# Neighbourhood attention of a two-block model: score and value matmuls of two heads issued in turn on the two halves of the array

## What is computed

```python
s_loc = jnp.einsum('bcqhd,brcmhd->bhcqrm', q_r, kb)          # 256 band keys
s_loc = jnp.where(col_valid, s_loc + bias, NEG_INF)
s_ctx = jnp.einsum('bcqhd,blhd->bhcql', q_r, kc)             # 256 context keys
p = jax.nn.softmax(jnp.concatenate([s_loc, s_ctx], -1), -1)
out = einsum(p_loc, vb) + einsum(p_ctx, vc)
```

## Time and profile before

| | us |
|---|---|
| median of 3 runs | 1833.73 |
| lowest, highest | 1828.89, 1835.4 |
| the profiled execution, whole | 1830.14 |
| its span, first to last instruction | 1828.5 |

### The profile page before, as it was taken

The page is one execution under the profiler, slowest core; times in us unless marked ns, Lnnn a source line. Parts: engine busy times, 40 slices in busy tenths (PEclk is TensorE's granted clock), DMA queues, the critical chain, the costliest instruction groups (busy, mean ns, idle before and its releaser), DMA issues.

```text
span 1828.5 us, 22256 instructions
## 1 busy us (share of the span) xinstructions
PE 1789.1 (98%) x8184; PEld 1441.1 (79%) x8184; DVE 973.3 (53%) x1237; ACT 676.2 (37%) x945; POOL 187.5 (10%) x170
## 2 busy tenths in 40 slices
PE   8999999999999999999999999989999999999999
PEld 6888888877887777876888888866787777788887
DVE  4333358866764664556433333346867768654442
ACT  4232222244344355534323222135444445632221
POOL 0000001122204602012000000003010020000000
PEclk9999999988999999999999999999999999999999
DMA  5232346613112334222322233221222222133331
GB/s 201 92 103 92 102 161 206 200 36 119 56 58 70 116 115 153 77 69 71 114 93 102 93 102 100 100 76 64 90 92 67 92 77 81 46 127 106 103 105 67
DMA packets 50315, 182.68 MB, mean 100 GB/s; under 512 B 5648, under 2 KB 5904, under 8 KB 50000
## 3 DMA queue, kind: packets, MB, share of 16 engines
q1 hardware_dynamic: 44352, 161.50, 26.5%
q10 hardware_dynamic: 4896, 14.96, 2.4%
q0 software_dynamic: 1008, 5.41, 0.9%
HBM read 179.75 MB, written 2.10 MB: 99 GB/s over the span
## 4 chain that ended last, share of the span: by engine, by line
PE 90%; DVE 5%; ACT 2%; issue 2%; DMA 0%; DVEq 0%; ACTq 0%
PE proj L364 79%; PE aux L467 2%; PE aux L1334 1%; DVE w_lo L356 1%; PE aux L1316 1%; PE aux L1324 1%; PE aux L1133 1%; ACT w_hi L349 1%; DVE y L1490 1%; PE aux L690 1%; PE proj L1154 1%; PE aux L1317 1%; DVE h L502 1%; DVE a_lo L506 0%; ACT md L812 0%
## 5 line engine op out<-in xcount | busy, mean ns | idle before, releaser
L356 DVE TENSOR_TENSOR w_lo<-raw,w_hi 128x1024 fp32r<-128x1024 f32 x304 | 405.4, 1335 | 457.4 <-ACT w_hi L349 450.4
L364 PE MATMUL proj<-a_hi,w_hi 128*128 128x512 f32 x1504 | 597.1, 397 | 16.3 <-DVE a_lo L1839 8.9
L364 PE MATMUL proj<-a_hi,w_lo 128*128 128x512 f32 x1504 | 588.4, 391 | 0.0
L364 PE MATMUL proj<-a_lo,w_hi 128*128 128x512 f32 x1504 | 588.2, 391 | 0.0
L349 ACT ACTIVATE w_hi<-raw 128x1024 fp32r<-128x1024 f32 x304 | 319.8, 1053 | 283.4 <-PE proj L364 245.4
L364 PEld LDWEIGHTS proj<-a_hi,w_hi 128*128 128x128 f32 x1504 | 284.1, 189 | 86.2 <-issue 25.9
L364 PEld LDWEIGHTS proj<-a_lo,w_hi 128*128 128x128 f32 x1504 | 284.2, 189 | 60.5 <-issue 2.6
L364 PEld LDWEIGHTS proj<-a_hi,w_lo 128*128 128x128 f32 x1504 | 283.9, 189 | 59.8
L364 PE MATMUL proj<-hid_hi,w_lo 128*128 128x512 f32 x352 | 139.0, 395 | 0.0
L364 PE MATMUL proj<-hid_hi,w_hi 128*128 128x512 f32 x352 | 139.0, 395 | 0.0
L364 PE MATMUL proj<-hid_lo,w_hi 128*128 128x512 f32 x352 | 139.0, 395 | 0.0
(11 more groups left out here) (295 smaller groups left out, 2067.6 us busy)
## 6 DMA issues: line engine op xcount, KB each, us to landing
raw<-stream SPq DMA_DIRECT2D x304, 512.0 KB, 3.4
ctxk<-ada_in ACTq DMA_DIRECT2D x12, 512.0 KB, 3.5
ctxv<-ada_in ACTq DMA_DIRECT2D x12, 512.0 KB, 3.4
h<-x_in SPq DMA_DIRECT2D x4, 512.0 KB, 7.1
out<-h ACTq DMA_DIRECT2D x8, 256.0 KB, 2.0
btab<-rpb_in POOLq DMA_DIRECT2D x4, 384.0 KB, 3.5
side<-mem_in POOLq DMA_DIRECT2D x1, 1024.0 KB, 5.0
side<-ctx_in POOLq DMA_DIRECT2D x1, 1024.0 KB, 6.2
```

Of the source, the lines that this page charges most:

```text
L356: nc.vector.tensor_tensor(w_lo[:, st.slot], raw[:, st.slot], w_hi[:, st.slot].bitcast(F32), ALU.subtract).then_inc(lo_ready, 1)
L364: mm = nc.tensor.matmul(dst, a, b, start=start and n == 0, stop=stop and n == 2)
```

## The change

`scores(u)` becomes `scores_of_pair(u)`, which issues the band matmuls of head 0 and head 1 and then their context matmuls. It stands where scores(a+2) stood; scores(a+3), which stood behind turn(a+1), is gone from there. The pair waits for the exps of both earlier units instead of one at each. `values(u)` becomes `values_of_pair(u)`, which goes over the four blocks and issues head 0 and head 1 for each. Its wait is for the later of the two units' turned. No matmul is added or taken away, and the lists of DVE, ACT, POOL and SP are the same.

```diff
-            def scores(u):
-                cb, lo = u // 2, HD * (u % 2)
-                part = slice(lo, lo + HD)
+            def scores_of_pair(u):
+                cb = u // 2
+                heads = [slice(0, HD), slice(HD, 2 * HD)]
                 if u == 0:
...
-                if u >= 2:
-                    pe.wait_ge(u_exp, u - 1 + UN * i)
-                q = nq[part, cb * P:(cb + 1) * P]
-                nc.tensor.matmul(aux[:, u % 2, :M], q, grid(nk[part], ROWS, BAND_AT[cb], BAND), start=True, stop=True)
-                nc.tensor.matmul(aux[:, u % 2, M:], q, ck_c[part], start=True, stop=True).then_inc(u_sc, 1)
+                else:
+                    pe.wait_ge(u_exp, u + UN * i)
+                at = slice(cb * P, (cb + 1) * P)
+                for n, part in enumerate(heads):
+                    nc.tensor.matmul(aux[:, n, :M], nq[part, at], grid(nk[part], ROWS, BAND_AT[cb], BAND), start=True,
+                                     stop=True)
+                for n, part in enumerate(heads):
+                    nc.tensor.matmul(aux[:, n, M:], nq[part, at], ck_c[part], start=True, stop=True).then_inc(u_sc, 1)
...
-            def values(u):
-                cb, lo = u // 2, HD * (u % 2)
-                pe.wait_ge(u_pt, u + 1 + UN * i)
+            def values_of_pair(u):
+                cb = u // 2
+                pe.wait_ge(u_pt, u + 2 + UN * i)
...
                 for b in range(4):
-                    v = vband[:, 2 * cb + b, lo:lo + HD] if b < 2 else cv_c[:, b - 2, lo:lo + HD]
-                    mm = nc.tensor.matmul(aux[lo:lo + HD, 3, cb * P:(cb + 1) * P], v, npt[:, u % 2, b * P:(b + 1) * P],
-                                          start=(b == 0), stop=(b == 3))
-                mm.then_inc(u_pv, 1)
+                    for n in range(2):
+                        lo = HD * n
+                        v = vband[:, 2 * cb + b, lo:lo + HD] if b < 2 else cv_c[:, b - 2, lo:lo + HD]
+                        mm = nc.tensor.matmul(aux[lo:lo + HD, 3, cb * P:(cb + 1) * P], v,
+                                              npt[:, n, b * P:(b + 1) * P], start=(b == 0), stop=(b == 3))
+                        if b == 3:
+                            mm.then_inc(u_pv, 1)
...
                 if 8 <= j <= 11:
-                    values(a - 2)
-                    values(a - 1)
+                    values_of_pair(a - 2)
                 if 6 <= j <= 9:
-                    scores(a + 2)
+                    scores_of_pair(a + 2)
                 if 7 <= j <= 10:
                     turn(a + 1)
-                if 6 <= j <= 9:
-                    scores(a + 3)
```

## The result

| | before | changed |
|---|---|---|
| median, us | 1832.94 | 1810.9 |
| lowest to highest | 1828.89 to 1835.4 | 1809.93 to 1812.27 |
| profiled execution | 1830.14 | 1811.72 |
| its span | 1828.5 | 1810.1 |

Four runs each. The ratio is 0.989, with a 95% interval of 0.9879 to 0.9902: faster by 1.1% (the two medians of the table are 22.0 us apart, 1.2%). The forecast was 1813 us with a range of 1806 to 1820, and 1810.9 was measured. The two profiled spans differ by 18.4 us. This is less than the change took from its stage, and the rows show why.

A forecast was written before the change was run, and what follows sets the result against it. PE, 98% busy, was taken to bound the kernel. Scores 15.0 plus values 5.8 less a 0.6 wait gave 20.2 us, so 1813 us from the 1833.7 median, range 1806 to 1820.

The forecast's parts named there:

- The stage's sum: Neighbourhood stage: 15.0 us from scores plus 5.8 from values less 0.6 of waiting, 20.2 us shorter.
- Scores: Pairs split by a turn at j = 7, 8, 9: joining them saves 1.25 us at 12 places, 15.0 us.
- Values: Alternating value pairs take 1.03 instead of 1.51 us; 0.48 us each for 12 pairs at j = 8, 9, 11: 5.8 us.
- The four pairs at j = 10: Value pairs before turn(7), which waits for ACT's turned(6): gain 0.
- The wait in the first group: PE reaches turn(2) before DVE's norm(2) ends in the first group and waits 0.6 us, once.
- Cover: DVE's norm(2) for i = 1 ends 0.3 us before PE reaches turn(2), growing by 0.2 us a round.
- (1): Second head starts late, scores losing 3.6 us and values 1.4: 1818 us; chance 0.08.
- (2): Values gain nothing because the two column halves share weight loading: 1819 us; chance 0.05.
- The rule of the Trainium skill: Weight loads overlap running matmuls only in different row groups, matmuls run strictly in order: values gain 0, sum 14.4 us.
- (3): DVE becomes the bound; a chain 0.4 us longer a round loses some 4 us over the turns: 1817 us; chance 0.03.
- (4): Slower: each change of half costs a drain, 27 us lost in values and scores' gain shrinking to 2.4: 1863 us; chance 0.03.
- (5): No overlap behind a turn, only 2.4 us left from the saved array-shape change: 1831 us; chance 0.03.

The follow-up runs named there:

- e1: Kernel before with scores(a+3) moved directly behind scores(a+2), head after head, each with its own wait; 1817.6 against 1830.8 us, ratio 0.993.
- e2: Kernel before with only the values of two heads alternating, scores still split by the turn; 1824.5 against 1830.8 us, ratio 0.9969.
- e5: Changed kernel with two DVE convolution taps moved from step 9 to steps 7 and 8; stage 291.2 us against 286.55.
- e3: Changed kernel with the values of a pair head after head behind the one wait; stage 292.3 us against 286.55.
- e4: Changed kernel with values alternating by two blocks, four load-and-matmul pairs of a head at a time; stage 287.2 us against 286.55.
- e10: Changed kernel with values as three blocks of head 0, three of head 1, then the last of each; stage 289.9 us against 286.55.
- e9: Changed kernel with head 1's scores computed from head 0's queries and keys, both on rows 0 to 63; stage 298.5 us against 286.55.

## Why the prediction was right, point by point

- **The stage's sum.** Forecast 20.2, measured 20.3 us in the profiles, 20.1 of it from the first scores on. The agreement to 0.1 us is partly luck, since a profile's stage is good to 0.4 us. The sum held because both terms had a row of the trace for the very thing that was to come: the score pair after strip 6, and the second half of a value pair.
- **Scores.** 15.0 us forecast before the wait, 14.4 after it; e1 alone gave 14.4. The pieces: 1.06 us a pair (1.07), 0.42 us from turn to strip (0.38), the strip behind a turn 0.02 us shorter, which was not in the sum.
- **Values.** 1.03 forecast, 1.03 measured; 5.8 forecast, 5.9 by e2. The four pairs at j = 10 gave nothing, for the reason that was given.
- **The wait in the first group.** From the strip's start to turn(2) it is 6.17 us there, 0.6 more than the 5.56 elsewhere; forecast 0.6. The profile calls 0.47 us of it idle time for norm.
- **Cover.** norm(2) of i = 1 ends at 1379.36 and turn(2) starts at 1379.64, a cover of 0.28 (0.3); e5 shows that it is real.
- **The total.** The forecast on the median was 1813.5, 2.6 us above what came: the medians moved by more than the stage. The median of before had been 1833.7 by three runs and is 1832.9 by four. The rest is as large as the 2 us by which the part in front of the stage varies, but that it is this is not shown, as the other runs have no profile. That the total came within 3 us owes something to luck, since this spread is not in the sum.
- **Rivals.** (1), a late second head, is true of the values in the old order but not of four pairs: e3, e4 and e10 show where it begins. (2) fell with e2, whose value pairs take 1.03 us. The rule of the Trainium skill that the prediction sets against the trace ("TensorE: Matmul & The Clock Gate", "Part 3: Packing small matmuls — row/col tiling"), on weight loads and strict order, does not agree with these runs either: the values, which use all rows, gained 5.9 us, and in e3 head 1's first matmul starts at 1380.06, ahead of one of head 0 at 1380.16. (3) did not come, by the margin that e5 measured. (4) and (5) did not come. Both use 2.4 us for the scores without overlap, from two separate heads at 2.11 us; with the 1.92 that e9 measured it is (1.64 - 0.38 - 0.86) x 12 = 4.8 us, so (5) would have been about 1829 us.
- **A slip.** The chances of the forecast and of rivals (1) to (3) add up to 0.94 and that of (5) is 0.03, where the prediction's last figures have 0.93 and 0.04. Nothing rests on it.

What the words of the change suggest, that alternation gives the gain, is true of 5.9 of 20.3 us only.

## What to carry to other kernels

Before packing small matmuls by hand, look in the timeline whether neighbours on different halves already overlap: moving two such groups next to each other may be most of the gain. In this kernel alternation paid only where more than four load-and-matmul pairs of one half stood in a row (six and eight lost time, four next to nothing; five was not tried). Then read how long before its use the next input is ready, since a faster PE eats into this cover (here 0.3 us are left). And where PE waits anyway, as in front of turn(7), shortening what stands before the wait gives nothing: put other work there first.

## What the runs showed of the hardware that was not expected

- The second half's first matmul starts once only three unstarted load-and-matmul pairs of the other half stand in front of it: 0.49 us late behind eight pairs (before and e3), 0.27 behind six (e10), 0.01 behind four (e4). Within one half the order of the list holds, between the halves it does not. These are pairs of float32 matmuls of 128 columns in one kernel; other shapes were not tried.
- A semaphore wait between the two heads, already met, costs the overlap nothing (e1, 1.07 us a score pair; in e3 the wait is taken away and the value pair takes 1.52 us, as with it).
- The same eight matmuls of 64 rows cost 1.06 us on two halves and 1.92 on one (e9).
- A TensorE that is busy throughout does not have the same clock throughout: near 390 us it issues matmuls of one column (line 690), without a gap, and the granted clock goes from 1.00 (385 to 391 us) to 0.50 (391.3 to 401.3) before; in the changed kernel it is 1.00 from 385 to 389.3 us and 0.50 from 389.7 to 403. So moment and length differ between executions of the same instructions, which is part of the 2 us in front of the stage.
